# Feed-forward up projection by Strassen's scheme: seven block products in place of eight for 20 of 22 tile pairs

## The reference

```python
def conv_ffn(h, w_up, conv_w, conv_b, w_down):
    up = h @ w_up
    s_len = up.shape[1]
    padded = jnp.pad(up, ((0, 0), (CONV_WIDTH_2 - 1, 0), (0, 0)))
    conv = conv_b + padded[:, 0:s_len] * conv_w[0]
    for j in range(1, CONV_WIDTH_2):
        conv = conv + padded[:, j:j + s_len] * conv_w[j]
    gate, val = jnp.split(conv, 2, axis=-1)
    return (jax.nn.silu(gate) * val) @ w_down
...
        x = x + conv_ffn(rms_norm(x, norm2_g[l]), w_up[l], conv_w[l], conv_b[l], w_down[l])
```

## Time and profile before

| | us |
|---|---|
| median of 3 runs | 3634.87 |
| lowest, highest | 3626.18, 3640.45 |
| span of the profiled execution | 3637.2 |
| PE busy in it | 3500.9 |
| DVE, POOL, ACT busy | 1833.4, 1786.0, 921.9 |

### The profile page before, as it was taken

How to read it: one execution, slowest core, us unless ns; L and a number is a source line. 1 busy time by engine, 2 the same in 40 slices (tenths; PEclk the granted TensorE clock), 3 DMA queues, 4 the chain that set the end, 5 groups by cost and what they waited for, 6 DMA issues and landing times.

```text
span 3637.2 us, 50803 instructions
## 1 busy us (share of the span) xinstructions
PE 3500.9 (96%) x20352; PEld 2804.6 (77%) x20352; DVE 1833.4 (50%) x2481; ACT 921.9 (25%) x1487; POOL 1786.0 (49%) x1798
## 2 busy tenths in 40 slices
PE   5998999999899999999999999998999999999998
PEld 3886788877678777877788888876787788888886
DVE  5684834559482366335535335354444543444346
ACT  4113643221363333232211111113223220111111
POOL 3342013666303378448744444556746854444445
PEclk8999999999999999999999999999999999999999
DMA  5510001331001243214211111113312311111113
GB/s 211 214 53 12 2 31 40 116 118 54 12 2 37 73 153 112 64 59 128 76 47 41 55 50 41 56 55 128 99 53 82 117 55 56 53 38 56 49 37 100
DMA packets 87611, 257.59 MB, mean 71 GB/s; under 512 B 9808, under 2 KB 12880, under 8 KB 86736
## 3 DMA queue, kind: packets, MB, share of 16 engines
q1 hardware_dynamic: 70896, 216.58, 17.9%
q10 hardware_dynamic: 16480, 37.76, 3.5%
HBM read 229.14 MB, written 16.78 MB: 68 GB/s over the span
## 4 chain that ended last, share of the span: by engine, by line
PE 81%; DVE 9%; POOL 5%; ACT 2%; issue 1%; DMA 1%; SPq 0%; DVEq 0%; POOLq 0%; ACTq 0%
PE banks L692 22%; PE banks L693 22%; PE banks L694 21%; POOL w_lo L2484 3%; DVE wk L1989 3%; PE banks L825 2%; PE banks L839 2%; PE banks L858 2%; DVE nt L1894 1%; POOL w_hi L2481 1%; DVE h_lo L1907 1%; DMA gw<-w_mod 1%; PE banks L853 1%; DVE h_lo L1910 1%; DVE nt L1883 1%
## 5 line engine op out<-in xcount | busy, mean ns | idle before, releaser
L692 PE MATMUL banks<-h_hi,w_hi 128*128 128x512 f32 (+1 forms) x3440 | 1338.4, 389 | 13.1 <-POOLq L2489 11.9
L693 PE MATMUL banks<-h_lo,w_hi 128*128 128x512 f32 (+1 forms) x3440 | 1321.2, 384 | 0.0
L694 PE MATMUL banks<-h_hi,w_lo 128*128 128x512 f32 (+1 forms) x3440 | 1320.2, 384 | 0.0
L2484 POOL TENSOR_TENSOR w_lo<-raw,w_hi 128x256 fp32r<-128x256 f32 x1320 | 1268.6, 989 | 31.2
L2481 POOL CAST w_hi<-raw 128x1024 fp32r<-128x1024 f32 (+2 forms) x390 | 397.6, 1019 | 1662.5 <-PE banks L694 1195.1
L692 PEld LDWEIGHTS banks<-h_hi,w_hi 128*128 128x128 f32 x3440 | 648.4, 188 | 167.7 <-POOLq L2489 26.4
L693 PEld LDWEIGHTS banks<-h_lo,w_hi 128*128 128x128 f32 x3440 | 648.6, 189 | 135.6 <-issue 7.5
L694 PEld LDWEIGHTS banks<-h_hi,w_lo 128*128 128x128 f32 x3440 | 648.1, 188 | 128.0
L2429 DVE TENSOR_SCALAR nt<-wk,v 128x1024 f32<-128x1024 f32 x88 | 90.0, 1023 | 461.9 <-ACTq L1826 435.5
L1605 ACT ACTIVATE wk<-banks 128x512 f32<-128x512 f32 x200 | 119.1, 596 | 707.0 <-PE banks L694 681.5
L692 PE MATMUL banks<-g_hi,w_hi 128*128 128x512 f32 x704 | 278.8, 396 | 9.4 <-DVEq L2418 6.8
(11 more groups left out here) (240 smaller groups left out, 3422.6 us busy)
## 6 DMA issues: line engine op xcount, KB each, us to landing
raw<-w_in SPq DMA_DIRECT2D x118, 512.0 KB, 3.3
raw<-w_ffn SPq DMA_DIRECT2D x96, 512.0 KB, 3.3
raw<-w_out SPq DMA_DIRECT2D x64, 512.0 KB, 3.3
raw<-w_down SPq DMA_DIRECT2D x96, 256.0 KB, 2.6
x<-w_mod SPq DMA_DIRECT2D x16, 1024.0 KB, 7.2
wk<-residual ACTq DMA_DIRECT2D x42, 256.0 KB, 2.9
gw<-w_mod SPq DMA_DIRECT2D x4, 2048.0 KB, 21.0
residual<-x ACTq DMA_DIRECT2D x4, 2048.0 KB, 10.4
```

The costliest lines, as they stand in the source:

```text
L692: mm(o, wh[:, ws], hi[:, at_, t0:t0 + n], start=kt == 0, stop=False)
L693: mm(o, wh[:, ws], lo[:, at_, t0:t0 + n], start=False, stop=False)
L694: last = mm(o, wl[:, ws], hi[:, at_, t0:t0 + n], start=False, stop=kt == nk - 1)
L2484: last = G.tensor_tensor(w_lo[:, piece], raw[:, piece], w_hi[:, piece].bitcast(F32), ALU.subtract)
```

## The change

The weights of a pair are read as a 2 x 2 matrix of blocks (gate, value) x (feature tiles 0 to 3, 4 to 7), the activations as (feature half) x (token half). Winograd's form of Strassen's scheme gives the four block results from seven products of 12 matmuls in place of eight. The first two pairs (`F0`) stay as they were.

Four sums of the activations (`t1_raw` to `t4_raw`, 2048 columns each) are made once per layer by VectorE, rounded by ScalarE and split by VectorE. Four sums of the weights (`s1_`, `s2_`, A11-A21 in place, `s4_`) are made for each pair by VectorE (`weight_sums`). Products 4, 5 and 6 accumulate in PSUM on top of products 0, 2 and 3 in banks 3, 5 and 6; before that, ScalarE (`take_first`) or VectorE (`take_middle`) must have read what the bank holds. Taps, product and low part now run in token halves of 512 (`convolve`).

The order is now a list of units (`UNITS`): an up unit is a pair, a down unit two pairs of g; down units follow f = 3 and every even f from 4 to 18, with the last two split by token half. A unit's weights (1 MB) are loaded by one DMA into one of two buffers (`pair_of`, `load_pair`); GpSimd splits them in blocks of 512 columns, seven for an up unit and four for a down unit, into a ring of three. `g` has three slots and one more for f = 21. Down results use four banks (`DOWN_BANKS`). The tables of the later stages give up the place that `pair_y` and a slot of g take, and one of them (1 MB) is loaded again between the layers. Several semaphores are merged.

```diff
-GROUPS = [(0, 4), (4, 8), (8, 12), (12, 16), (16, 18), (18, 22)]
-LAST = len(GROUPS) - 1
-NG = 6
-AFTER = {4: 0, 8: 1, 12: 2, 16: 3, 21: 4}
+F0 = 2
+def units():
+    seq = []
+    for f in range(F0, NF):
+        seq.append(("up", f, None))
+        if f == 3:
+            seq.append(("down", 0, (0, 1)))
+        elif f % 2 == 0 and 4 <= f <= 18:
+            seq.append(("down", f // 2 - 1, (0, 1)))
+    for p in range(2):
+        seq += [("down", 9, (p,)), ("down", 10, (p,))]
+    return seq
+UNITS = units()
+UP_UNIT = {f: n for n, (kind, f, _) in enumerate(UNITS) if kind == "up"}
...
+U_BLOCK = np.cumsum([0] + [7 if u[0] == "up" else 4 for u in UNITS]).tolist()
...
+BLOCK_END = np.cumsum(BLOCK_RESULTS).tolist()
+DOWN_BANKS = (0, 1, 2, 7)
...
+    def pair_of(n):
+        return raw if n % 2 else pair_y
...
+            def load_pair(l, n):
+                kind, i, _ = UNITS[n]
...
+                elif n >= 2:
+                    sp.wait_ge(sem["block_ready"], l * N_BLOCK + U_BLOCK[n - 1])
...
+                if kind == "up":
+                    src, c = w_ffn[l, 2 * i:2 * i + 2].rearrange("m p c -> p m c"), 1024
+                else:
+                    src, c = w_down[l, :, :, 2 * i * P:2 * (i + 1) * P].rearrange("d p c -> p d c"), 256
+                sp.dma_start(pair_of(n)[:, :].rearrange("p (m c) -> p m c", c=c), src).then_inc(sem[f"u_in{n % 2}"], 16)
...
+                def products(n, f):
...
+                    b11, b21, b22, t4 = h2(0, 0), h2(4, 0), h2(4, 512), h2(0, 512)
...
+                    def product(i, moving, bank, first):
+                        b = N_BLOCK * l + U_BLOCK[n] + i
+                        pe.wait_ge(sem["block_ready"], b + 1)
+                        o = b % 3 * 512
+                        for kt, (hi, lo) in enumerate(moving):
+                            ws = slice(o + kt * P, o + (kt + 1) * P)
+                            mm(psum[bank], w_hi[:, ws], hi, start=first and kt == 0, stop=False, skip_group_check=True)
+                            mm(psum[bank], w_hi[:, ws], lo, start=False, stop=False, skip_group_check=True)
+                            last = mm(psum[bank], w_lo[:, ws], hi, start=False, stop=kt == 3, skip_group_check=True)
+                        last.then_inc(sem["result_ready"], 1)
+                    if u:
+                        pe.wait_ge(sem["taken_act"], 2 * u)
+                    product(0, b11, 3, True)
+                    if u:
+                        pe.wait_ge(sem["taken_dve"], 5 * u - 4)
+                    if f == F0:
+                        pe.wait_ge(sem["t_split"], 4 * l + 2)
+                    product(1, t2, 4, True)
+                    if u:
+                        pe.wait_ge(sem["taken_dve"], 5 * u - 1)
+                    product(2, t1, 5, True)
+                    if u:
+                        pe.wait_ge(sem["taken_dve"], 5 * u)
+                    if f == F0:
+                        pe.wait_ge(sem["t_split"], 4 * l + 4)
+                    product(3, t3, 6, True)
+                    pe.wait_ge(sem["taken_act"], 2 * u + 1)
+                    product(4, b21, 3, False)
+                    pe.wait_ge(sem["taken_dve"], 5 * u + 2)
+                    product(5, b22, 5, False)
+                    pe.wait_ge(sem["taken_dve"], 5 * u + 3)
+                    product(6, t4, 6, False)
...
+                def down(n, g, halves, sums=None):
+                    pe.wait_ge(sem["g_ready"], NF * l + 2 * g + 2)
...
                     for d in range(DT):
...
+                        if d % 2 == 0:
+                            pe.wait_ge(sem["block_ready"], b + 1)
...
+                        for p in halves:
+                            if c >= 4:
+                                pe.wait_ge(sem["down_free"], c - 3)
...
+                            for kt in range(2):
+                                ws, f = slice(o + kt * P, o + (kt + 1) * P), 2 * g + kt
+                                mm(bank, w_hi[:, ws], g_part(f, 0, p), start=kt == 0, stop=False)
+                                mm(bank, w_hi[:, ws], g_part(f, 1, p), start=False, stop=False)
+                                last = mm(bank, w_lo[:, ws], g_part(f, 0, p), start=False, stop=kt == 1)
+                            last.then_inc(sem["result_ready"], 1)
...
+                def gate_silu(f, h):
+                    act.wait_ge(sem["ff_conv"], 2 * (NF * l + f) + h + 1)
+                    A(ff_c[0], ff_c[0], ACT.Silu).then_inc(sem["ff_gated"], 1)
+                def round_g(f, h):
+                    act.wait_ge(sem["ff_prod"], 2 * (NF * l + f) + h + 1)
...
+                    A(g_part(f, 0, h), ff_c[1], ACT.Copy).then_inc(sem["ff_hi"], 1)
+                def take_first(f):
...
+                    act.wait_ge(sem["result_ready"], N_RESULT * l + U_RESULT[UP_UNIT[f]] + 1)
+                    if u:
+                        act.wait_ge(sem["taken_dve"], 5 * u)
+                    A(ff_u, psum[3], ACT.Copy).then_inc(sem["taken_act"], 1)
+                def take_second(f):
+                    act.wait_ge(sem["result_ready"], N_RESULT * l + U_RESULT[UP_UNIT[f]] + 5)
+                    if f > F0:
+                        act.wait_ge(sem["ff_conv"], 2 * (NF * l + f))
+                    A(ff_up(f, 0)[:, 2:514], psum[3], ACT.Copy).then_inc(sem["taken_act"], 1)
...
+                for f in range(F0, NF):
+                    between = UNITS[UP_UNIT[f] - 1][0] == "down"
+                    if f == F0:
+                        take_first(f)
+                    gate_silu(f - 1, 0)
+                    if f > F0 and not between:
+                        take_first(f)
+                    round_g(f - 1, 0)
+                    gate_silu(f - 1, 1)
+                    round_g(f - 1, 1)
+                    if f > F0 and between:
+                        take_first(f)
+                    take_second(f)
...
+                def weight_sums(f):
...
+                    a11, a12, a21, a22 = [pair[:, i * 512:(i + 1) * 512] for i in range(4)]
+                    dve.wait_ge(sem[f"u_in{n % 2}"], pair_loads(l, n))
+                    if f > F0:
...
+                        last_sum(f)
...
+                def last_sum(f):
...
+                    link(V.tensor_tensor(s4_[:, :], a12, s2_[:, :], ALU.subtract))
+                    dve.sem_inc(sem["sums_ready"], 1)
...
+                link(V.tensor_tensor(t1_raw, second1, first1, ALU.subtract))
+                link(V.tensor_tensor(t3_raw, second2, second1, ALU.subtract))
+                link(V.tensor_tensor(t2_raw, second2, t1_raw, ALU.subtract))
+                link(V.tensor_tensor(t4_raw, first2, t2_raw, ALU.subtract))
+                dve.sem_inc(sem["sums_ready"], 1)
+                weight_sums(F0)
+                for i, raw_t in enumerate((t1_raw, t2_raw)):
+                    dve.wait_ge(sem["t_hi_ready"], 4 * l + i + 1)
+                    V.tensor_tensor(t_lo[i][:, :], raw_t, t_hi[i][:, :].bitcast(F32), ALU.subtract).then_inc(sem["t_split"], 1)
...
+                def take_down(n, c, final=None):
...
+                    dve.wait_ge(sem["result_ready"], N_RESULT * l + U_RESULT[n] + c + 1)
...
+                    link(V.tensor_tensor(xs, psum[DOWN_BANKS[q % 4]], xs, ALU.add))
+                    dve.sem_inc(sem["down_free"], 1)
...
+                    def taps(m, h):
+                        u, c, wi, o = ff_up(f, m), ff_c[m], 22 * m + f, 512 * h
+                        link(V.tensor_scalar(c, u[:, o + 2:o + 514], w2("conv_w", 88 + wi), w2("conv_b", wi), ALU.mult, ALU.add))
+                        add_some()
...
+                    taps(0, 0)
+                    taps(1, 0)
+                    gate(0)
+                    taps(0, 1)
+                    low(0)
+                    taps(1, 1)
+                    gate(1)
+                    low(1)
...
+                convolve(0)
+                dve.wait_ge(sem["acc_ready"], end_q)
+                last_sum(F0)
+                dve.wait_ge(sem["t_hi_ready"], 4 * l + 3)
+                V.tensor_tensor(h2_lo[:, 0:4, 512:S], four(t4_raw), h2_hi[:, 0:4, 512:S].bitcast(F32), ALU.subtract).then_inc(sem["t_split"], 1)
+                dve.wait_ge(sem["t_hi_ready"], 4 * l + 4)
+                V.tensor_tensor(t_lo[2][:, :], t3_raw, t_hi[2][:, :].bitcast(F32), ALU.subtract).then_inc(sem["t_split"], 1)
...
+                def take_middle(f):
...
+                    dve.wait_ge(sem["taken_act"], 2 * u + 1)
+                    link(take(f, 1, ff_u, 4))
+                    dve.sem_inc(sem["taken_dve"], 1)
+                    both = ff_up(f, 1)[:, 514:1026]
+                    link(take(f, 2, both, 5))
+                    dve.sem_inc(sem["taken_dve"], 1)
+                    if f < NF - 1:
+                        weight_sums(f + 1)
+                    dve.wait_ge(sem["result_ready"], N_RESULT * l + U_RESULT[UP_UNIT[f]] + 4)
+                    link(V.tensor_tensor(both, psum[6], both, ALU.add))
+                    dve.sem_inc(sem["taken_dve"], 1)
```

(108 more changed lines are left out.)

365 lines of the change are left out of this document (198 added, 167 removed).

## The result

The changed kernel takes **3809.05 us** (median of 4, 3799.7 to 3811.7) against 3635.57 us before on the same chip: ratio 1.0474, 95% interval 1.0453 to 1.0495. Forecast were 3900 us, between 3720 and 3980. The time lies in the range and on the forecast side. The size is 173 us instead of 268: outside the likeliest stretch of 3860 to 3980, and among rival 1's values.

A forecast was written before the change was run, and what follows sets the result against it. TensorE's matmuls were taken to bound the kernel, busy 96% of 3637.2 us. Net terms of 73 + 28 + 5 + 2 - 2.7 + 12 + 13 + 4 = 134 us per layer, twice, gave 3905, about 3900 us; range 3720 to 3980.

The forecast's parts named there:

- rival 1: Feed-forward stage: VectorE's queue still decides, but without the lower clock or with few meetings; 3700 to 3860 us, chance 30%.
- meetings: GpSimd and VectorE operations running at once in the feed-forward stage lengthen each other; each costs a tap 0.36 us.
- the second pair: Second of two consecutive pairs before a down unit (even f, 6 to 18): 33 us, seven times per layer.
- The second wait: In the second pair, product 6 waits behind the load, weight sums and VectorE's read of product 3: 5.4 us.
- low clock: In the second pair, after TensorE's waits the clock drops to 1.2 GHz; product 6 ends some 2.4 us later.
- The down unit: Down projection: VectorE alternates convolution and take, 1.67 us a step; ends at 24.1 us, 22.3 without meetings.
- f = 4 and f = 19 to 21: Pairs, per layer: f = 4 waits for its load, +5 us; f = 19 -2.7; f = 20 and 21 +7 and +5.
- the tail: Stage end, per layer: second down group waits for g of f = 21, +13 us; last pass +4.
- The start: Early tiles to f = 3: VectorE's sums, low parts and convolutions hold products; +28 us per layer, 15 without meetings.
- Rival 2: Faster: in the second pair VectorE's take 2 and the load finish in time, TensorE sets the pace; 3575 us, 7%.
- Rival 3: Each of the meetings costs a tap all of GpSimd's 0.70 us; about 60 us per layer, 4020 us, chance 3%.
- the 60 of the bound: Sign that the prediction is wrong: TensorE's waits in the feed-forward stage sum to under 60 us.

The follow-up runs named there:

- Experiment 3: Changed kernel without GpSimd's differences for the low parts of the new units' weights (old values kept; casts, loads and matmuls stay): 3705.2 us, ratio 1.0198.
- experiment 12: Kernel of 11 without GpSimd's differences for the low parts of the new units' weights (old values kept): 3592.7 us, ratio 0.9897.
- experiment 9: Kernel of experiment 4; in pairs following a pair, VectorE takes products 2 and 3 behind the value half's taps, before the gate half's last taps: 3734.4 us.
- experiment 4: Changed kernel with takes 1 and 2 before the old pair's last gate product and low part, and weight sums behind take 3: 3734.2 us, ratio 1.0281.
- 11: Kernel of experiment 9 with reordered start and tail, and two down results instead of one behind each convolution instruction in down units: 3705.15 us, ratio 1.0200.

## Why the prediction was right, and where it was off

**Direction and cause: right.** VectorE's queue sets the pace, GpSimd makes it longer. Product 5 was forecast at 20.3 us after product 0; it came at 20.4 (2038.40 - 2018.00). That it fits to 0.1 us is partly luck: in f = 8 the queue without meetings would take 15.5 us, not 14.9, and its 16 operations pay 4.9 us, not 5.4 (each record against its time alone). Experiment 3 took the meetings with GpSimd's differences away and 104 of 173 us went with them; experiment 12, with the orders mended, crossed below the kernel before. The share that the forecast gave to meetings and clock together was (134 - 31) x 2 = 206 of 268 us.

**The step that failed: the size of the second pair.** 33 us were forecast, 28.0 measured on average (27.6 to 28.7), seven times per layer, the larger part of the 95 us between forecast and result. The second wait in it, behind the load and the sums, did not come. Three terms of it:
- Block 6 was put at 18.1 us; it was split at 15.2 (load issued at 2033.24). I had let every GpSimd operation meet a VectorE one and pay; GpSimd's measured mean is 0.90 us, not 1.1.
- The load took 4.9 us, not 5.5, so it had landed at 20.1 and not at 23.6, and the sums did not wait for it. The four weight sums met nobody: they run while GpSimd waits for product 5. I charged 4.0 us for 3.0. So take 3 came at 24.3 instead of 28.4 us.
- I let product 6 wait for it as a second wait of 5.4 us, with 2.4 us of low clock behind it. With product 5 starting at 20.4 and running slowly to 25, a take at 24.3 is hidden behind it. In the seven second pairs of layer 0 product 6 never waits. The low clock cost 1.7 to 2.8 us in them, on product 5 and the start of product 6, near the 2.4 of the forecast.

**The down unit**: 24.1 forecast, 22.3 to 23.0 measured, the lower bound given. Behind an add the next tap waits 0.15 us, behind a tap the next add only 0.03, so a step is 1.42 us with a first tap (0.55 + 0.15 + 0.69 + 0.03) and 1.62 with one of the eight others, in the mean 1.55 and not 1.67. The bound is real all the same: with all of the convolution in it, experiment 9 shows 27.0.

**The other places.** f = 4 and f = 19 to 21 are within 1 us per layer. In the tail the wait is 10.7 us for 13, but the tail as a whole +20.8 for +17; the rest of it I have not taken apart. The start is +22.5 for +28, and not quite as told: product 3 of f = 2 came 14 us after the early tiles instead of 22, and the wait before f = 3 (8.6 us) fell on its product 0, which ScalarE's second evacuation of f = 2 holds (L1984), not on its product 2. VectorE's `convolve(1)` stands ahead of that evacuation, as the forecast had it for the two takes. **Missed** are 8.9 us per layer in the early tiles: I priced what GpSimd does to VectorE's long sums and not what the long sums do to GpSimd, which still feeds the old projections. The end of each layer (+2.7 in layer 0, +6.5 in layer 1) was taken as +4, inside the tail.

**The rivals.** Rival 1's value came true, its mechanism only in part: waits and meetings are there, the clock too, but fewer things add up. Rival 2 (faster) needed taps a third shorter; with taps at 0.76 instead of 0.95 us, a fifth, experiment 3 is still slower, and only with the order changed too does experiment 12 cross over. Rival 3 (a meeting costs the whole instruction of the other engine) is wrong for VectorE, which pays 0.42 us for a difference of 0.70. It is right for GpSimd, 10.85 us for four differences beside instructions of 2.7. The Trainium skill ("SBUF — State Buffer", Who interferes with whom) calls what the two share an exclusive lock: the trace agrees with it for what GpSimd waits, not for what VectorE pays.

**Of the signs that were named**, those of the 480 matmuls, TensorE's share, the wait behind take 2, VectorE's share of the stage (75%) and the wait in the tail came true. The waits on products 5 and 6 sum to 141 us over both layers, above the 60 of the bound. Wrong: the taps' mean is 0.95 and that of GpSimd's differences 0.90, not 1.1, and the clock digits of the stages are 8 and 9, not 6 to 8. And VectorE's sums waited for a load of `w_ffn` only at f = 3 and 4 (2.5 and 7.3 us in layer 0), in none of the 14 second pairs; that sign stood for the second wait, the step that failed.

**Open.** How much of experiments 3 and 12 comes from GpSimd's own shorter queue was not separated. Whether another engine for the differences, or fewer and wider VectorE instructions, would keep what experiment 12 shows was not tried. Nor was a longer or shorter spell of the lower clock by itself. The best complete version is 2.0% slower than the kernel before.

## What to carry to other kernels

A cut in matmuls pays only if the engines that prepare and fetch for them have room after their own additions: here 12 matmuls less (2.75 us) cost VectorE nine operations and its old ones in halves, and each VectorE instruction that meets GpSimd pays its 0.4 us again, so count instructions, not elements. When one in-order queue feeds several waits, mend the whole order at once: moving takes 1 and 2 forward alone only moved the wait (3 us), moving the sums back alone gave 19, both gave 75. And look at both sides of a meeting: beside long VectorE instructions it was GpSimd that waited (10.85 us instead of 2.84 for four differences), beside short ones VectorE paid more in all.

## What the runs showed of the hardware

- VectorE and GpSimd alternate by instructions: one 256-column difference per VectorE instruction, of 512 columns (four differences in 4.49 us) or of 2048 (10.85 us). Each VectorE instruction pays 0.42 us at either length (0.69 to 1.11, 2.29 to 2.70).
- In f = 8 the granted clock fell to 1.2 GHz 3.5 us into a wait of 6.5 us and stayed there 6.9 us; with the waits of 3.0 us in experiment 4 the mean over two pairs is 0.96, and in experiments 9, 11 and 12, with none inside the pairs, 1.00.
- Loads of 1024 KB landed in 4.9 us (`w_ffn`) and 5.4 us (`w_down`), less than twice the 3.3 us of 512 KB.
